# Attention with decay: the order of transposes, scores and projection steps within a head

## The chip, the cores and the metric

The kernel runs on one core of a Trainium2 chip, as one program. The metric is the time of one execution on the device, in microseconds (us). A profile of one execution shows five engines: TensorE (PE in the rows; its weight loads stand apart as PEld), VectorE (DVE), ScalarE (ACT), GpSimd (POOL) and SyncE (SP), which here only issues transfers.

## The reference, cut to what matters

The program computes two blocks of a network for 1024 tokens of width 1024. The change lies in the last layer of the second block, in its attention with decay ("forgetting attention"): 16 heads of width 64, causal, with a learned decay that is added to the scores.

```python
def forgetting_attention(u, k, v, cum):
    q = u.reshape(B, S, FOX_HEADS, FOX_HEAD_DIM)
    ...
    def block(args):
        qi, ci, s0 = args
        logits = jnp.einsum('bqhd,bkhd->bhqk', qi, k,
                            preferred_element_type=jnp.float32) * scale
        logits = logits + (ci[..., :, None] - cum_k[:, :, None, :])
        qpos = s0 + jnp.arange(Q_BLOCK)
        mask = kpos[None, :] <= qpos[:, None]
        logits = jnp.where(mask[None, None], logits, -jnp.inf)
        p = jax.nn.softmax(logits, axis=-1)
        return jnp.einsum('bhqk,bkhd->bqhd', p.astype(v.dtype), v)
```

The queries, keys and gates of each head come from projections of the layer's input `x`, by columns of `w_in` and `w_kv_shared`.

## The kernel before, in words

All matrices are split into a high and a low part, so that one product of two of them is three matmuls (`mm3`, L437 to L439). Every engine has its own program, written out by hand in a fixed order, and the programs meet at semaphores. Nothing schedules anything at run time: an engine whose next instruction has to wait stands still, and all that is behind it waits too.

The loop over the 16 heads (stage "fox") runs on TensorE, ScalarE and VectorE side by side. A head has eight tiles of 128 queries, `qt` 0 to 7. Tile `qt` sees `qt + 1` blocks of 128 keys, in one chunk of up to 512 keys for tiles 0 to 3 and in two for tiles 4 to 7. A tile goes through this chain:

1. `scores` (TensorE, L1767, L1768, and L1770 for the causal mask) writes a chunk to one of three PSUM banks.
2. `row_max` (VectorE, L3121) adds the decay, finds the extreme of each row and writes the logits to `tmp`, of which there are two, one for even and one for odd tiles.
3. `exps` (ScalarE, L1907, `tmp<-tmp,mx`) takes the exponential in place and its row sum.
4. `flips` (TensorE, L1781) transposes the exponentials block by block, one matmul each, to one of two PSUM banks.
5. `flip_hi` (ScalarE, `ET.._hi<-ps`) and `flip_lo` (VectorE, L2426, `ET.._lo<-ps`) split the transposed block.
6. `values` (TensorE, L1799) multiplies two tiles at a time (pair p is tiles 2p and 2p + 1) with the values, once both are split. `other_half` (ScalarE, `tmp<-ps 64x256`) and `add` (VectorE, L2429) bring the sum to `Y`, and free the bank of the next pair.

Between these TensorE has other work to fill its time: projection steps for later heads, `fill(n)` in units of one step, three matmuls of 512 columns. Eight steps make a half tile, a head has 24 steps, and the table `FILL` says how many stand at each of ten places: behind the scores of tiles 0 to 7, and around the last transposes. Heads 14 and 15 have less to project and go by `FILL_LAST`. A half tile for keys and queries (`kq`) is brought in by three ScalarE instructions (`project`) and three on VectorE, the last of them a cast (L3093); one for a gate takes one and one. Of these, the one finished at the end of the head before is brought in at tile 0, the first of this head at tile 2, the second from tile 5 on. In even heads from 2 on the one at tile 0 is a `kq` one; the one at tile 2 is `kq` in all even heads and a gate in odd ones. GpSimd splits the next weights (L881, `whi`, and L883, `wlo`) when a panel comes free, once of these at the end of each odd head.

The orders that matter are the three loops over `qt`, one on each engine, which must agree with each other.

Of the kernel before, what the change touches and what calls it, by code (L numbers as in the profile page):

```python
# [99 lines left out]
def chunks_of(qt):  # L100
    return 1 if qt < 4 else 2
# [62 lines left out]


MERGE_SPLITS = (4, 6, 8, 10)
FILL = (4, 4, 4, 3, 2, 1, 2, 1, 2, 1)
FILL_LAST = (3, 3, 3, 3, 2, 2, 0, 0, 0, 0)
VORDER = (tuple(range(8)), (2, 3, 4, 5, 6, 7, 0, 1))

# [46 lines left out]
def build(nc, d, out, upto=99, dbg=None):  # L217
    ctx = ExitStack()
    with ctx:
# [798 lines left out]
        def pe_program(pe):  # L1018
# [124 lines left out]
            if on("gates"):  # L1143
# [14 lines left out]
                def fill(n):  # L1158
                    for _ in range(n):
                        next(tiles, None)  # L1160
# [554 lines left out]
            if on("fox"):  # L1715
# [29 lines left out]
                def half_tiles(h):  # L1745
                    for kind, x, s in projections(h):
                        yield from half_tile(half_panel(kind, x), s)
# [69 lines left out]
                for h in range(FOX):  # L1817
                    steps = half_tiles(h)
                    share = FILL if h < FOX - 2 else FILL_LAST

                    def fill(n):
                        for _ in range(n):
                            next(steps, None)

                    for qt in range(8):
                        scores(h, qt)
                        if qt == 7:
                            fill(share[qt])
                        if qt:
                            flips(h, qt - 1)  # L1830
                        if qt < 7:
                            fill(share[qt])
                        if qt in (3, 5, 7):
                            values(h, qt // 2 - 1)
                        elif qt == 1 and h:
                            values(h - 1, 3)
                    fill(share[8])
                    if h == FOX - 1:
                        next(ahead)
                    flips(h, 7)  # L1840
                    fill(share[9])
                    if h == FOX - 1:
                        next(ahead)
# [61 lines left out]
        def act_program(act):  # L1905
# [167 lines left out]
            if on("mla"):  # L2073
# [18 lines left out]
                def exps(t):  # L2092
                    x = 8 * (t // 8 % 2) + t % 8
                    act.wait_ge(S("ml_max"), t + 1)
                    copy(tmp3[t % 3][:, :], tmp3[t % 3][:, :], S("ml_e"), ACT.Exp, bias=neg_max[:, x:x + 1], accum_out=row_sum[:, x:x + 1])
# [247 lines left out]
            if on("fox"):  # L2343
                def project(kind, x, s):

                    c = slice(HALF * s, HALF * s + HALF)
                    m = half_panel(kind, x)
                    if s:
                        panels_done(act, "fox", 25, 0, m)
                    else:  # L2350
                        act.wait_ge(S("fx_half"), m + 1)
                    g = ps[:, (6 + s) * HALF:(7 + s) * HALF]
                    if kind == "kq":
                        j = x % 2
                        if x < 2:
                            act.wait_ge(S("fx_vst"), 16)
                        else:
                            act.wait_ge(S("fx_x"), CHUNKS * (x - 1))
                        copy(K1[j][0:64, c], g[0:64, :], S("fx_kqa"))
                        copy(Q1[j][64:128, c], g[64:128, :], S("fx_kqa"), scale=64 ** -0.5)  # L2360
                        act.wait_ge(S("fx_kqa"), 4 * x + 2 * s + 1)
                        copy(K1[j][64:128, c], f32(K1[j][0:64, c]), S("fx_ka2"))
                    elif kind == "mq":
                        copy(Qm[0][0][:, c], g, S("mq_hi"))
                    else:
                        act.wait_ge(S("gate_log"), 4)
                        if x >= 2:
                            act.wait_ge(S("fx_yg"), x - 1)
                        copy(SG[x % 2][:, c], g, S("fx_sig"), ACT.Tanh, scale=0.5)

                def exps(h, qt):
                    x = 8 * (h % 2) + qt
                    act.wait_ge(S("fx_x"), CHUNKS * h + first_chunk(qt) + chunks_of(qt))
                    e = tmp[qt % 2][:, 0:P * qt + P]
                    copy(e, e, S("fx_e"), ACT.Exp, scale=-1.0, bias=neg_max[:, x:x + 1], accum_out=row_sum[:, x:x + 1])

                def flip_hi(h, qt):
                    p = qt // 2
                    if 4 * h + p >= 2:
                        act.wait_ge(S("fx_out"), 3 * (4 * h + p) - 5)  # L2380
                    for x in range(chunks_of(qt)):
                        n = CHUNKS * h + first_chunk(qt) + x
                        k0, k1 = 4 * x, min(4 * x + 4, qt + 1)
                        act.wait_ge(S("fx_t"), n + 1)
                        b = (3 + n % 2) * HALF
                        if qt == 0 and h:
                            act.wait_ge(S("row_stored"), CUM_STORED + 16 * (h - 1))
                            copy(inv_rows, ps[0:8, b + P:b + 2 * P], S("fx_inv"))
                        copy(ET[p % 2][0][:, k0:k1, P * (qt % 2):P * (qt % 2) + P], ps[:, b:b + P * (k1 - k0)].rearrange("p (k q) -> p k q", q=P), S("fx_hi"))

                def other_half(h, p):
                    o = others(64 * (h % 2))
                    r = slice(64 * (h % 2), 64 * (h % 2) + 64)
                    act.wait_ge(S("fx_out"), 3 * (4 * h + p) + 1)
                    copy(other[r, :], ps[o, 5 * HALF:5 * HALF + CTX], S("fx_out"))

                for x in (("kq", 0, 0), ("kq", 0, 1), ("gate", 0, 0), ("gate", 0, 1)):
                    project(*x)
                for h in range(FOX):
                    before = projections(h - 1)[2:] if h else []  # L2400
                    mine = projections(h)[0:2]
                    for qt in range(8):
                        if qt:
                            flip_hi(h, qt - 1)
                        exps(h, qt)
                        if qt in (3, 5, 7):
                            other_half(h, qt // 2 - 1)
                        elif qt == 1 and h:
                            other_half(h - 1, 3)
                        if qt == 0:  # L2410
                            for x in before:
                                project(*x)
                        if qt in (2, 5) and mine:
                            project(*mine[qt // 4])
                    flip_hi(h, 7)
                other_half(FOX - 1, 3)
# [6 lines left out]
        def dve_program(dve):  # L2423
# [655 lines left out]
            if on("fox"):  # L3079
# [69 lines left out]
                for h in range(FOX):  # L3149
                    before = projections(h - 1)[2:] if h else []  # L3150
                    mine = projections(h)[0:2]
                    for qt in range(8):
                        for x in range(chunks_of(qt)):
                            row_max(h, qt, x)
                        for x in range(chunks_of(qt - 1) if qt else 0):
                            flip_lo(h, qt - 1, x)
                        if qt in (3, 5, 7):
                            add(h, qt // 2 - 1)
                        elif qt == 1 and h:
                            add(h - 1, 3)  # L3160
                        if qt == 0:
                            for x in before:
                                project(*x)
                        if qt == 2 and mine:
                            project(*mine[0])
                        if qt >= 5 and mine:
                            kind, which, half = mine[1]
                            if kind == "kq":
                                keys_queries(which, half, qt - 5)
                            elif qt == 5:  # L3170
                                project(kind, which, half)
                        if qt == 7 and h % 2 == 0 and h:
                            gate(h // 2 - 1)
                    x = slice(8 * (h % 2), 8 * (h % 2) + 8)
                    dve.wait_ge(S("fx_e"), 8 * h + 8)
                    if h:
                        dve.wait_ge(S("fx_inv"), 2 * h)
                    nc.vector.reciprocal(inv_sum[:, x], row_sum[:, x]).then_inc(S("fx_inv"), 1)
                    for x in range(2):
                        flip_lo(h, 7, x)  # L3180
# [148 lines left out]
```

## Time and profile before

| | |
|---|---|
| median of 3 executions | 3017.0 us (3014.71 to 3017.37) |
| the profiled execution | 3021.57 us |
| its span, first to last instruction | 3019.8 us |
| TensorE busy | 2916.5 us, 97% of the span |
| VectorE, ScalarE, GpSimd busy | 49%, 31%, 37% |
| granted TensorE clock, mean | 0.991 of full speed |

The span is the profile's own time, and 1.8 us of the execution lie around it. TensorE is busy nearly always, so its instructions set the time; where it stands still, the chain that it waits for does.

### The profile page before, as it was taken

How to read it: one execution, taken by the hardware profiler on the slowest of the kernel's cores; microseconds unless marked ns; L12 is line 12 of the kernel's file. 1: busy time of each engine (PE TensorE's matmuls, PEld its weight loads, DVE VectorE, ACT ScalarE, POOL GpSimd, SP SyncE). 2: the span in 40 equal slices, each digit the busy share in tenths (PEclk: the TensorE clock that was granted, in tenths of full speed). 3: DMA queues.
4: the chain of work that ended last, by engine and by line, in shares of the span. 5: the costliest groups of instructions: out<-in, count | busy, mean ns of one | idle time of the engine just before them, and what ended most of it. 6: DMA issues, size and time to landing. Idle time of an engine off the chain costs nothing. (4 is left out here: it accounts for less than half of the span.)

```text
span 3019.8 us, 37184 instructions
## 1 busy us (share of the span) xinstructions
PE 2916.5 (97%) x14772; PEld 2424.8 (80%) x14772; DVE 1491.6 (49%) x2202; ACT 925.3 (31%) x1628; POOL 1108.4 (37%) x585
## 2 busy tenths in 40 slices
PE   7999999999999999999999999999899999999997
PEld 3877778888887888888888887788788888887786
DVE  5842237887644313122133444445626666664545
ACT  4122226675113101010011111420326555653411
POOL 1332351111586434444443443234343233322241
PEclk9999999999999999999999999999999999999998
DMA  5534574331533111111111111111142222221111
GB/s 239 188 129 142 191 235 137 86 89 48 190 122 112 50 49 49 49 50 49 50 49 49 49 63 56 42 42 49 54 165 63 73 66 71 69 71 50 37 49 63
DMA packets 123821, 263.00 MB, mean 87 GB/s; under 512 B 48476, under 2 KB 74540, under 8 KB 119424
## 3 DMA queue, kind: packets, MB, share of 16 engines
q1 hardware_dynamic: 123648, 260.57, 26.2%
q8 instruction: 124, 2.03, 0.3%
q14 instruction: 49, 0.40, 0.0%
HBM read 215.97 MB, written 46.06 MB: 87 GB/s over the span
## 5 line engine op out<-in xcount | busy, mean ns | idle before, releaser
L881 POOL TENSOR_TENSOR whi<-raw,onesf 128x1024 fp32r<-128x1024 f32 x187 | 362.0, 1936 | 1313.1 <-PE ps L439 1208.9
L437 PE MATMUL ps<-Hb_hi,whi 128*128 128x512 f32 x1424 | 572.6, 402 | 10.3 <-DVE Y L2846 5.9
L439 PE MATMUL ps<-Hb_hi,wlo 128*128 128x512 f32 x1424 | 556.0, 390 | 0.0
L438 PE MATMUL ps<-Hb_lo,whi 128*128 128x512 f32 x1424 | 554.9, 390 | 0.0
L883 POOL TENSOR_TENSOR wlo<-raw,whi 128x1024 fp32r<-128x1024 f32 x187 | 499.3, 2670 | 14.6
L437 PEld LDWEIGHTS ps<-Hb_hi,whi 128*128 128x128 f32 x1424 | 267.9, 188 | 62.6 <-issue 8.3
L439 PEld LDWEIGHTS ps<-Hb_hi,wlo 128*128 128x128 f32 x1424 | 267.2, 188 | 57.7
L438 PEld LDWEIGHTS ps<-Hb_lo,whi 128*128 128x128 f32 x1424 | 268.3, 188 | 48.0
L1907 ACT ACTIVATE tmp<-ps 64x256 f32<-64x256 f32 (+3 forms) x112 | 61.8, 552 | 535.9 <-PE ps L439 465.1
L1907 ACT ACTIVATE tmp<-tmp,mx 128x1280 f32<-128x1280 f32 (+2 forms) x192 | 187.1, 974 | 79.8 <-DVE mx L3121 50.3
L439 PE MATMUL ps<-Uhi,wlo 128*128 128x512 f32 x512 | 199.2, 389 | 0.0
L437 PE MATMUL ps<-Uhi,whi 128*128 128x512 f32 x512 | 199.2, 389 | 0.0
L438 PE MATMUL ps<-Ulo,whi 128*128 128x512 f32 x512 | 199.2, 389 | 0.0
L2429 DVE TENSOR_TENSOR tmp<-tmp 128x1024 f32<-128x1024 f32 x44 | 86.1, 1957 | 184.1 <-ACT tmp L1907 183.7
L2793 DVE SCALAR_TENSOR_TENSOR X<-ps,modx,X 128x1024 f32<-128x1024 f32 x32 | 41.1, 1283 | 256.6 <-PE ps L439 256.6
L437 PE MATMUL ps<-Yb_hi,whi 128*128 128x512 f32 (+1 forms) x408 | 153.8, 377 | 0.0
L438 PE MATMUL ps<-Yb_lo,whi 128*128 128x512 f32 (+1 forms) x408 | 153.6, 377 | 0.0
L439 PE MATMUL ps<-Yb_hi,wlo 128*128 128x512 f32 (+1 forms) x408 | 153.6, 377 | 0.0
L437 PE MATMUL ps<-Hhi,whi 128*128 128x512 f32 x384 | 151.8, 395 | 0.4 <-ACT ql L1907 0.2
L438 PE MATMUL ps<-Hlo,whi 128*128 128x512 f32 x384 | 149.6, 390 | 0.0
L439 PE MATMUL ps<-Hhi,wlo 128*128 128x512 f32 x384 | 149.5, 389 | 0.0
L438 PEld LDWEIGHTS ps<-Ulo,whi 128*128 128x128 f32 x512 | 96.1, 188 | 20.1
(468 smaller groups left out, 5832.4 us busy)
## 6 DMA issues: line engine op xcount, KB each, us to landing
raw<-in_w SPq DMA_DIRECT2D x197, 512.0 KB, 3.5
adas<-in_ada SPq DMA_DIRECT2D x16, 1024.0 KB, 4.9
raw<-in_w SPq DMA_DIRECT2D x44, 256.0 KB, 3.7
adaE<-in_ada SPq DMA_DIRECT2D x4, 2048.0 KB, 23.2
gate_d<-gst SPq DMA_DIRECT2D x16, 512.0 KB, 2.8
v_d<-VS SPq DMA_DIRECT2D x2, 4096.0 KB, 14.2
ncB<-cum_d SPq DMA_DIRECT2D x16, 512.0 KB, 3.6
Vx<-v_d SPq DMA_DIRECT2D x16, 512.0 KB, 3.8
```

What stands on the lines that cost most here:

```text
L437: nc.tensor.matmul(o, wh, xh, start=start, stop=False)
L438: nc.tensor.matmul(o, wh, xl, start=False, stop=False)
L439: return nc.tensor.matmul(o, wl, xh, start=False, stop=stop)
L881: nc.gpsimd.tensor_tensor(whi[b][:, 0:w], raw[b][:, 0:w], onesf[:, 0:1].to_broadcast([P, w]), ALU.mult).then_inc(S("split_hi"), 1)
L883: nc.gpsimd.tensor_tensor(wlo[b][:, 0:w], raw[b][:, 0:w], f32(whi[b][:, 0:w]), ALU.subtract).then_inc(S("split"), 1)
L1907: nc.scalar.activation(dst, src, func, **kw).then_inc(sem, 1)
L2429: nc.vector.tensor_tensor(o, a, b, op).then_inc(sem, 1)
L2793: nc.vector.scalar_tensor_tensor(X1[:, k, :], g, modx[:, 40 + k:41 + k], X1[:, k, :], ALU.mult, ALU.add).then_inc(free, 1)
```

## The change

The transposes of tile `t` stood behind the scores of tile `t + 1`, and the projection steps of that place behind them. Now the table `FLIPPED` places them: those of tiles 0 and 1 stand together behind the scores and the steps of tile 1, those of tiles 2 and 3 together behind the scores and the steps of tile 3. Behind the scores of tile 4 stand no transposes. Those of tiles 4, 5, 6 and 7 stay where they were. ScalarE and VectorE follow the same order, and on ScalarE the exponential of tiles 1 to 4 now comes ahead of the `flip_hi` that stand at the same place. `FILL` is redistributed (24 steps, as before); `FILL_LAST` stays.

```diff
--- before.py
+++ after.py
@@ -164,7 +164,8 @@
 
 
 MERGE_SPLITS = (4, 6, 8, 10)
-FILL = (4, 4, 4, 3, 2, 1, 2, 1, 2, 1)
+FILL = (3, 4, 3, 4, 2, 1, 2, 1, 2, 2)
+FLIPPED = {1: (0, 1), 3: (2, 3), 5: (4,), 6: (5,), 7: (6,)}
 FILL_LAST = (3, 3, 3, 3, 2, 2, 0, 0, 0, 0)
 VORDER = (tuple(range(8)), (2, 3, 4, 5, 6, 7, 0, 1))
 
@@ -1824,11 +1825,11 @@
 
                     for qt in range(8):
                         scores(h, qt)
-                        if qt == 7:
+                        if qt < 4 or qt == 7:
                             fill(share[qt])
-                        if qt:
-                            flips(h, qt - 1)
-                        if qt < 7:
+                        for t in FLIPPED.get(qt, ()):
+                            flips(h, t)
+                        if 4 <= qt < 7:
                             fill(share[qt])
                         if qt in (3, 5, 7):
                             values(h, qt // 2 - 1)
@@ -2400,9 +2401,12 @@
                     before = projections(h - 1)[2:] if h else []
                     mine = projections(h)[0:2]
                     for qt in range(8):
-                        if qt:
-                            flip_hi(h, qt - 1)
-                        exps(h, qt)
+                        if qt < 5:
+                            exps(h, qt)
+                        for t in FLIPPED.get(qt, ()):
+                            flip_hi(h, t)
+                        if qt >= 5:
+                            exps(h, qt)
                         if qt in (3, 5, 7):
                             other_half(h, qt // 2 - 1)
                         elif qt == 1 and h:
@@ -3152,8 +3156,9 @@
                     for qt in range(8):
                         for x in range(chunks_of(qt)):
                             row_max(h, qt, x)
-                        for x in range(chunks_of(qt - 1) if qt else 0):
-                            flip_lo(h, qt - 1, x)
+                        for t in FLIPPED.get(qt, ()):
+                            for x in range(chunks_of(t)):
+                                flip_lo(h, t, x)
                         if qt in (3, 5, 7):
                             add(h, qt // 2 - 1)
                         elif qt == 1 and h:
```

TensorE, head 2, from the last two matmuls of the values of pair 0 to the first projection step of tile 4 (`Vx` values, `K` keys, `Q` queries, `mrow` the causal mask, `Hb` and `w` the projections). Before:

```order
L1799 MATMUL ps<-ETa_hi,Vx_191 128x128
L1799 MATMUL ps<-ETa_lo,Vx_191 128x128
L1767 MATMUL ps<-K_0_187,Q_0_185 128x512
L1768 MATMUL ps<-K_0_189,Q_0_185 128x512
L1767 MATMUL ps<-K_0_187,Q_0_185 128x128
L1768 MATMUL ps<-K_0_189,Q_0_185 128x128
L1770 MATMUL ps<-mrow_60,identr 128x128
L1781 MATMUL ps<-ident,tmp 128x128 x4
L437 MATMUL ps<-Hb_hi,whi 128x512
```

And now, in the same head, where all line numbers are a little higher:

```order
L1782 MATMUL ps<-ident,tmp 128x128 x7
L1800 MATMUL ps<-ETa_hi,Vx_191 128x256
L1800 MATMUL ps<-ETa_lo,Vx_191 128x256
L1800 MATMUL ps<-ETa_hi,Vx_191 128x128
L1800 MATMUL ps<-ETa_lo,Vx_191 128x128
L1768 MATMUL ps<-K_0_187,Q_0_185 128x512
L1769 MATMUL ps<-K_0_189,Q_0_185 128x512
L1768 MATMUL ps<-K_0_187,Q_0_185 128x128
L1769 MATMUL ps<-K_0_189,Q_0_185 128x128
L1771 MATMUL ps<-mrow_60,identr 128x128
L438 MATMUL ps<-Hb_hi,whi 128x512
```

The four transposes of tile 3 moved from behind the scores of tile 4 to ahead of the values, where they join the three of tile 2.

VectorE, same head, from `row_max` of tile 3 to that of tile 4 (`ISA` is `row_max` or its second part, `ETb_lo` is `flip_lo`, `Y` is `add`). Before:

```order
L3121 ISA tmp,mx<-ps,ncB 128x512
L3121 ISA mx 128x1
L2426 TENSOR_TENSOR ETb_lo<-ps,ETb_hi 128x3x128
L2429 TENSOR_TENSOR Y_170<-ps,tmp 64x256
L3121 ISA tmp,mx<-ps,ncB 128x512
L3121 ISA mx 128x1
L3121 ISA tmp,mx<-ps,ncB,mx 128x128
L3121 ISA mx 128x1
L2426 TENSOR_TENSOR ETb_lo<-ps,ETb_hi 128x4x128
```

Now:

```order
L3125 ISA tmp,mx<-ps,ncB 128x512
L3125 ISA mx 128x1
L2430 TENSOR_TENSOR ETb_lo<-ps,ETb_hi 128x3x128
L2430 TENSOR_TENSOR ETb_lo<-ps,ETb_hi 128x4x128
L2433 TENSOR_TENSOR Y_170<-ps,tmp 64x256
L3125 ISA tmp,mx<-ps,ncB 128x512
L3125 ISA mx 128x1
L3125 ISA tmp,mx<-ps,ncB,mx 128x128
L3125 ISA mx 128x1
```

The low half of tile 3 moved from behind `row_max` of tile 4 to ahead of it and of the `add` of pair 0.

ScalarE, same head, from the key and query copies of tile 2's place to the exponential of tile 4 (`128x512` and `128x640` with `mxf` are the exponentials of tiles 3 and 4, `64x256` is `other_half`). Before:

```order
L1907 ACTIVATE K_1_188<-K_1_188 64x512
L1907 ACTIVATE ETb_hi<-ps 128x3x128
L1907 ACTIVATE tmp,mxf<-tmp,mx 128x512
L1907 ACTIVATE tmp<-ps 64x256
L1907 ACTIVATE ETb_hi<-ps 128x4x128
L1907 ACTIVATE tmp,mxf<-tmp,mx 128x640
```

Now:

```order
L1908 ACTIVATE K_1_188<-K_1_188 64x512
L1908 ACTIVATE tmp,mxf<-tmp,mx 128x512
L1908 ACTIVATE ETb_hi<-ps 128x3x128
L1908 ACTIVATE ETb_hi<-ps 128x4x128
L1908 ACTIVATE tmp<-ps 64x256
L1908 ACTIVATE tmp,mxf<-tmp,mx 128x640
```

The exponential of tile 3 went ahead of the high half of tile 2, and the high half of tile 3 ahead of `other_half`.

## Rows read from the trace of the kernel before

**Rows 1.** View of windows, head 6: length, busy time (xinstructions), PE clock, DMA share, GB/s.

```profile
2434.64:2465.00 30.36, 30.36 (x183) 26.66 (x181) 20.83 (x50) 18.90 (x43) 11.72 (x8) 1.00 0.26 79
```

**Rows 2.** View of waits, stretch of all heads: us in total, times, longest.

```profile
PE ps L1781 <- ACT tmp L1907: 4.1, 4, 1.2
```

**Rows 3.** Timeline of TensorE, head 6, tiles 4 and 5: start, duration, row, count.

```profile
2449.20 0.28 PE L1799 MATMUL ps<-ETa_hi,Vx 128*128 128x256 f32 x1
...
2449.60 0.45 PE L1767 MATMUL ps<-K,Q 128*128 128x512 f32 x1
...
2450.40 0.62 PE L1781 MATMUL ps<-ident,tmp 128*128 128x128 f32 x4
2450.78 0.47 PE L437 MATMUL ps<-Hb_hi,whi 128*128 128x512 f32 x1
2451.09 0.39 PE L438 MATMUL ps<-Hb_lo,whi 128*128 128x512 f32 x1
...
2452.25 0.40 PE L1767 MATMUL ps<-K,Q 128*128 128x512 f32 x1
...
2453.01 0.72 PE L1781 MATMUL ps<-ident,tmp 128*128 128x128 f32 x5
```

**Rows 4.** Timeline of ScalarE and VectorE, same stretch; in brackets idle before and releaser.

```profile
2449.81 0.38 ACT L1907 ACTIVATE tmp<-ps 64x256 f32<-64x256 f32 x1 [0.61 <-PE ps L1799]
...
2450.22 0.42 DVE L2429 TENSOR_TENSOR Y<-ps,tmp 64x256 f32<-64x256 f32 x1 [1.40 <-ACT tmp L1907]
...
2450.56 0.67 DVE L3121 CUSTOM_DVE_ANT_0 tmp<-ps,ncB 128x512 f32<-128x512 f32 x1
...
2451.12 0.60 ACT L1907 ACTIVATE ETb_hi<-ps 128x512 fp32r<-128x512 f32 x1 [0.93 <-PE ps L1781]
...
2451.75 0.69 DVE L2426 TENSOR_TENSOR ETb_lo<-ps,ETb_hi 128x512 fp32r<-128x512 f32 x1
2451.78 0.83 ACT L1907 ACTIVATE tmp<-tmp,mx 128x640 f32<-128x640 f32 x1
```

**Rows 5.** Timeline, exponentials and the transposes behind them, head 6 and head 15.

```profile
2458.57 1.05 ACT L1907 ACTIVATE tmp<-tmp,mx 128x896 f32<-128x896 f32 x1
...
2459.85 0.93 PE L1781 MATMUL ps<-ident,tmp 128*128 128x128 f32 x7
...
2708.72 0.40 ACT L1907 ACTIVATE tmp<-tmp,mx 128x128 f32<-128x128 f32 x1 [2.17 <-DVE mx L3121]
...
2709.26 0.33 PE L1781 MATMUL ps<-ident,tmp 128*128 128x128 f32 x1 [0.76 <-ACT tmp L1907]
```

**Rows 6.** Timeline of all engines, start of head 6.

```profile
2434.64 0.23 PE L1767 MATMUL ps<-K,Q 128*128 128x128 f32 x1
...
2434.93 0.45 PE L437 MATMUL ps<-Hb_hi,whi 128*128 128x512 f32 x1
...
2435.21 0.40 PE L438 MATMUL ps<-Hb_lo,whi 128*128 128x512 f32 x1
2435.44 0.39 PE L439 MATMUL ps<-Hb_hi,wlo 128*128 128x512 f32 x1
...
2436.93 2.40 POOL L883 TENSOR_TENSOR wlo<-raw,whi 128x1024 fp32r<-128x1024 f32 x1
...
2438.38 1.23 DVE L3093 CAST K<-K 64x512 fp32r<-64x512 f32 x1
...
2439.64 0.43 DVE L3121 CUSTOM_DVE_ANT_0 tmp<-ps,ncB 128x256 f32<-128x256 f32 x1
...
2440.11 0.51 ACT L1907 ACTIVATE tmp<-tmp,mx 128x256 f32<-128x256 f32 x1 [1.19 <-DVE mx L3121]
```

**Rows 7.** Timeline, head 6: scores of tile 2, a later cast, exponential of tile 3.

```profile
2442.86 0.39 PE L1767 MATMUL ps<-K,Q 128*128 128x384 f32 x1
...
2447.20 0.42 DVE L3093 CAST K<-K 64x512 fp32r<-64x512 f32 x1
...
2448.38 0.72 ACT L1907 ACTIVATE tmp<-tmp,mx 128x512 f32<-128x512 f32 x1 [0.50 <-DVE mx L3121]
```

## The prediction

> **What bounds the kernel now.** I read the windows first, by head. In head 6 TensorE is busy for all of its 30.36 us, at a granted clock of 1.00, while VectorE is busy 20.83 and ScalarE 18.90 [rows 1]. So a head lasts as long as the list of TensorE's instructions, and a change in order can help in two ways only: by taking away a wait of TensorE, or by making the same matmuls cheaper. Then the view of waits: over all 16 heads the transposes make TensorE wait for an exponential four times, 4.1 us in all [rows 2]. That is all that a better order could take from this wait. It can lose far more, since each of the 16 heads can get a new wait. So I went through the chains behind each wait of the new order, with the starts of one head from the timeline, and asked which instruction TensorE would reach before its input is there.
>
> A first price is needed: how soon behind an exponential its transposes can start. In head 15 TensorE really waited: the exponential started at 2708.72 and took 0.40, the transposes started at 2709.26, so 0.14 us behind its end. In head 6 the exponential of tile 6 started at 2458.57 and took 1.05, so its transposes could have started at 2459.76, and did at 2459.85 [rows 5]: on time, with 0.09 us to spare. The loop is tight already.
>
> **The change, place by place.** The transposes of tiles 5, 6 and 7 and their surroundings stay, so I cost four places.
>
> Tile 4, every head. Before, TensorE starts the transposes of tile 3 at 2450.40 and those of tile 4 at 2453.01, 2.61 us later, with two projection steps and the scores of tile 5 between them [rows 3]. Now the values of pair 0 (2449.20 to 2449.60, 0.40) and the scores of tile 4 (2449.60 to 2450.40, 0.80) stand between them as well [rows 3], and the mask's matmul is followed by a projection matmul, 0.06 (below). TensorE is there after 2.61 + 0.40 + 0.80 + 0.06 = 3.87 us.
>
> The chain that it then waits for begins at the same transposes of tile 3, which before had nothing to do with it. From 2450.40 it takes 0.72 to the high half (2451.12), which takes 0.60, and the low half starts at 2451.75, 1.35 behind the transposes [rows 3, 4]. Now `other_half` comes behind this high half, from 1.35 to 1.73; the low half takes 0.69, to 2.04; only then `add`, and `row_max` of tile 4 starts 0.34 behind the start of `add` (2450.22 to 2450.56), so at 2.07 + 0.34 = 2.41. From there it is 1.22 to the exponential (2450.56 to 2451.78) [rows 4]: 3.63. The exponential takes 0.83 and the step to the transposes 0.14: 4.60. TensorE is there at 3.87 and waits 0.73 us. In 16 heads this is 11.7 us, the largest term. Both ends: 0, if the scores of tile 4 were in fact not late for anything, which the rows exclude as long as `row_max` of tile 4 stands behind the low half and `add`; and 1.0 if each handover of the chain costs 0.05 more than where I read it. Behind the waiting transposes stand a projection step, the values of pair 1 and the scores of tile 6; nothing on the other engines runs ahead enough to make the time good, since they wait for these very transposes.
>
> Tile 1, even heads from 2 on. `row_max` of tile 1 stands on VectorE behind the three instructions that bring in keys and queries. In head 6 the last of these, a cast, starts at 2438.38 and takes 1.23, where the cast at 2447.20 takes 0.42 [rows 6, 7]. The difference is GpSimd: its `wlo` runs from 2436.93 to 2439.33, and the cast ends 0.28 behind it, at 2439.61 [rows 6]. GpSimd's two instructions hang on the last projection step of the head before, which still stands right ahead of the scores of tile 0. I take it that the cast, though it may start up to 0.7 us earlier by the table's extra step at the end of a head, is still held until `wlo` ends. Then `row_max` of tile 1 starts at 5.00 us from the head's start and the exponential at 5.47 as now; it takes 0.51, and the transposes of tile 1 can start at 6.12. TensorE gets there, with 0.29 for the scores of each of tiles 0 and 1, seven steps of 0.69 (a matmul follows the next by 0.23, 2435.21 to 2435.44), two masks at 0.06 and 0.15 for the transposes of tile 0 with the row sums, at 5.68 [rows 6]; the 0.29 for tile 1 and the 0.15 are estimates from tile 0 and from 0.38 for four transposes [rows 3]. The wait is 0.44, in heads 2 to 12 together 2.6 us. Head 14 goes by `FILL_LAST`, with one step less: 1.1 us. Ends: 0, if the cast is not held, and 0.7 for each.
> The Trainium skill says why, in SBUF — State Buffer, Who interferes with whom: a VectorE instruction that uses two ports and one of GpSimd take the shared pair of ports as a lock, and the later one stands still until the other has ended. The two casts agree with that. By this rule the sum holds the 3.7 us of this place; without it the casts would take 0.42 and the sum would be that much less.
>
> Tile 3, even heads. From the scores of tile 2 (2442.86) to the exponential of tile 3 (2448.38) it is 5.52, and 0.72 + 0.14 to its transposes: 6.38 [rows 7]. TensorE took 6.34 to the values of pair 0 (2449.20) [rows 3, 7]; now the transposes of tile 1 are no longer in it (two of 0.11), two masks add 0.12 and one handover of 0.06 falls away: 6.18. A wait of 0.20 in seven heads, 1.4 us, and 0.9 in head 14 with its shorter table. In odd heads a gate is brought in, one instruction for three, and there is none.
>
> The masks, every head. The last matmul of a tile's scores has 128 columns. Behind it the first matmul of a projection step takes 0.28 until the next (2434.93 to 2435.21), where it is 0.23 from the second to the third [rows 6]: some 0.06 that a matmul of 128 columns doesn't cover. Before, transposes stood behind four of these masks; now projection steps do, at tiles 1, 2, 3 and 4. Four times 0.06 in 16 heads would be 3.8 us; the transposes have the same exposed load in part, so I take 3 (ends 0 and 3.8).
>
> What is removed. Putting transposes together saves nothing that I can find: four take 0.38 and the matmul behind them 0.31 instead of 0.23 [rows 3, 6], 0.46 in all or 0.115 each, as if each were charged alone. The wait of head 15 for its first exponential, 0.76 [rows 5], goes, as four steps now lie ahead. No transfer is issued by these loops, and GpSimd and SyncE follow semaphores with time to spare; a later row of sums reaches them some 2 us later in a head of 30.
>
> Sum: 11.7 + 2.6 + 1.1 + 1.4 + 0.9 + 3.0 - 0.8 = 19.9 us. The profiled execution took 3021.57 (span 3019.8, 1.8 around it) and would take 3041; its time is 4.6 over the median of 3017.0, to which I add the same sum: 3037 us, 0.66% more.
>
> **The rivals.**
> The chain is longer than I read, and the new waits are not the last. The spare 0.09 us at tile 6 [rows 5] goes as soon as one copy is late, and then tile 6 waits in every head as well; with 0.25 there (4 us) and 1.0 instead of 0.73 at tile 4 (4.3 us) the time is 3045. For it: each engine's program is one queue, and every handover has its price. Against it: behind tile 4 all engines follow the same transposes, as before. Chance 0.2.
> The casts are not held at tile 1, as their start moves off GpSimd's work: 3.7 us less, 3033. Against it: GpSimd starts from the same projection step as before. Chance 0.1.
> The waits don't come, since ScalarE and VectorE, with 11 and 9 us of idle time in a head [rows 1], catch up. Then 3.0 - 0.8 remain, 3019, which can't be told from no change (0.2%, 6 us, is about what can be). Against it: idle time is no slack where a chain runs through it. Chance 0.07.
> It gets faster. The mechanism is the 0.08 that a matmul behind a group of transposes pays (0.31 against 0.23) [rows 3, 6]: if that is paid once for a group, two groups fewer in 16 heads save 2.6 us, and with the 4.1 us of waits [rows 2] gone, 6.7 us: 3010. It decides where the new waits stay under 0.4 us for each head. Against it: of those waits only the 0.76 stands at a place that changes, and tile 4's wait alone is above that bound. Chance 0.03.
>
> **How the numbers follow.** The forecast as worked out has 0.6, the rivals 0.2, 0.1, 0.07 and 0.03. The predicted time is 3037. The range runs from 3028, which takes in the casts that are not held and masks at nothing together with a fifth off the largest term, to 3047, which takes in the longer chain with the masks at 3.8 and is rounded up. Faster by over 0.2%: 0.03; within: 0.07; slower: 0.9.
>
> **What the profile would show.** Right: heads of some 31.3 us (odd) and 31.9 (even) instead of 30.4; in the view of waits, TensorE for an exponential at the transposes, 16 waits near 0.7 at tile 4, seven near 0.4 at tile 1, seven near 0.2 at tile 3; casts at tile 1 of even heads that end 0.28 behind `wlo`; projection matmuls at 0.28 behind masks. Wrong: no wait at tile 4, or `row_max` of tile 4 that starts within 2 us of the transposes of tile 3. The forecast fails if the distance between the transposes of tiles 3 and 4 is under 4 us.

## The result and the profile after

The changed kernel takes 3043.55 us (median of 4 executions, 3041.77 to 3047.2), the kernel before 3017.18 (4 executions, 3014.71 to 3022.37). The ratio is 1.0085, 95% interval 1.0071 to 1.0100: slower by 26 us, by 21 to 30. Forecast were 3037 us, with a range of 3028 to 3047, and 0.9 for slower.

The profiled execution took 3042.88 us with a span of 3041.1, 21.3 more than that of before. All of it lies in the heads; the rest of the span is 1.3 shorter. The view of windows over them, from the first scores of head 0 to the first matmul of the next stage (length, busy time of PE, PEld, DVE, ACT and POOL, then clock and transfers):

```profile
2251.55:2762.46 510.91, 491.83 (x2880) 424.03 (x2878) 318.17 (x771) 280.22 (x634) 147.56 (x108) 1.00 0.22 67
```

Before, this stretch took 488.29 us, from 2254.41 to 2742.70. It grew by 22.6. I call it the stage below and measure every kernel by it as well as by the ratio, since what lies outside it differs by some us from one profiled execution to another. Heads 6 and 7 of the changed kernel in the same view:

```profile
2439.62:2471.51 31.89, 31.23 (x183) 26.75 (x181) 21.33 (x51) 18.85 (x42) 11.51 (x8) 1.00 0.26 76
2471.51:2502.99 31.48, 30.73 (x182) 26.80 (x181) 18.61 (x49) 16.55 (x38) 7.22 (x6) 1.00 0.20 59
```

Head 6 took 30.36 us with TensorE busy throughout [rows 1]; now it takes 31.89 with 31.23 busy, and the odd head 7 takes 31.48 with 30.73 busy. ScalarE works no longer than before (18.85 against 18.90), and the granted clock is 1.00 as it was. TensorE runs the same matmuls and stands still between them. Its busy time grows as well (30.73 against 30.35 in head 7): the row of a matmul goes on after the next could have started, so a part of each wait counts as busy. The view of waits over the heads says what TensorE waits for:

```profile
PEld ps L1782 <- ACT tmp L1908: 26.3, 43, 1.4
...
PE ps L1782 <- ACT tmp L1908: 17.5, 30, 1.2
```

The wait for an exponential at the transposes grew from 4.1 us in 4 places [rows 2] to 17.5 in 30. The row of weight loads (PEld) shows the same waits once more, by the idle time of the loads; the two are not added. The largest one, at tile 4, in the timeline of TensorE for head 7:

```profile
2485.23 0.93 PE L1782 MATMUL ps<-ident,tmp 128*128 128x128 f32 x7
2485.91 0.36 PE L1800 MATMUL ps<-ETa_hi,Vx 128*128 128x256 f32 x1
...
2486.40 0.44 PE L1768 MATMUL ps<-K,Q 128*128 128x512 f32 x1
...
2488.61 0.39 PE L1768 MATMUL ps<-K,Q 128*128 128x512 f32 x1
...
2489.30 0.22 PE L1771 MATMUL ps<-mrow,identr 128*128 128x128 f32 x1
2490.28 0.77 PE L1782 MATMUL ps<-ident,tmp 128*128 128x128 f32 x5 [0.75 <-ACT tmp L1908]
```

From the mask (2489.30) to the transposes of tile 4 (2490.28) it is now 0.98 us, where an undisturbed mask is followed after 0.06; the 0.75 in brackets is only the part in which no matmul is busy. The wait costs 0.92 us. What it waited for, on ScalarE and VectorE:

```profile
2485.81 1.03 ACT L1908 ACTIVATE ETb_hi<-ps 128x384 fp32r<-128x384 f32 x2 [1.43 <-PE ps L1782]
2486.87 0.38 ACT L1908 ACTIVATE tmp<-ps 64x256 f32<-64x256 f32 x1
2489.30 0.83 ACT L1908 ACTIVATE tmp<-tmp,mx 128x640 f32<-128x640 f32 x1 [2.05 <-DVE mx L3125]
...
2486.34 1.23 DVE L2430 TENSOR_TENSOR ETb_lo<-ps,ETb_hi 128x384 fp32r<-128x384 f32 x2 [2.81 <-ACT ETb_hi L1908]
2487.60 0.43 DVE L2433 TENSOR_TENSOR Y<-ps,tmp 64x256 f32<-64x256 f32 x1
2488.06 0.69 DVE L3125 CUSTOM_DVE_ANT_0 tmp<-ps,ncB 128x512 f32<-128x512 f32 x1
```

The low halves of tiles 2 and 3 run as one row from 2486.34 to 2487.57; only then `add` (2487.60), `row_max` of tile 4 (2488.06) and its exponential (2489.30), and 0.98 behind its start the transposes. The scores of tile 4 had been there since 2487.4.

At tile 1 of an even head (GpSimd, VectorE, ScalarE, TensorE of head 6):

```profile
2441.90 2.40 POOL L884 TENSOR_TENSOR wlo<-raw,whi 128x1024 fp32r<-128x1024 f32 x1
...
2443.16 1.43 DVE L3097 CAST K<-K 64x512 fp32r<-64x512 f32 x1
2444.62 0.42 DVE L3125 CUSTOM_DVE_ANT_0 tmp<-ps,ncB 128x256 f32<-128x256 f32 x1
...
2445.09 0.51 ACT L1908 ACTIVATE tmp<-tmp,mx 128x256 f32<-128x256 f32 x1 [2.26 <-DVE mx L3125]
...
2445.74 0.44 PE L1782 MATMUL ps<-ident,tmp 128*128 128x128 f32 x2 [0.20 <-ACT tmp L1908]
```

GpSimd's `wlo` ends at 2444.30, the cast at 2444.59, and behind it `row_max`, the exponential and the transposes of tile 1, which are 0.43 us late (0.47 behind the row of sums where it was 0.10 in odd heads, and 0.20 to the values instead of 0.14). The cast started 3.54 us from the head's start instead of 3.74, and lasted 1.43 instead of 1.23 [rows 6], so it ended at the same place in the head.

At tile 3, TensorE of head 6, then GpSimd, VectorE and TensorE of head 8:

```profile
2453.77 1.15 PE L1782 MATMUL ps<-ident,tmp 128*128 128x128 f32 x7
2454.67 0.36 PE L1800 MATMUL ps<-ETa_hi,Vx 128*128 128x256 f32 x1
...
2515.29 0.73 POOL L898 TENSOR_TENSOR Y<-Y,rs 64x256 f32<-64x256 f32 x1 [7.61 <-DMA acc<-inv_d]
...
2515.57 0.73 DVE L3097 CAST K<-K 64x512 fp32r<-64x512 f32 x1
...
2517.94 0.66 PE L1782 MATMUL ps<-ident,tmp 128*128 128x128 f32 x4 [0.31 <-ACT tmp L1908]
```

The seven transposes of tiles 2 and 3 take 0.90 us in head 6, up to the values at 2454.67, and 0.68 in odd heads: 0.22 late. In head 8 the cast that stands ahead of `row_max` of tile 3 took 0.73 instead of 0.42: it ends at 2516.30, again 0.28 behind an instruction of GpSimd (a multiplication of the head before, 2515.29 to 2516.02). The transposes of tile 3 wait longer there and show 0.31 us of idle time.

### The profile page after: what moved, and what is told of

It is laid out like the page before. It is cut to its first block, busy times and chain, and to the rows that moved or that the text cites. A ratio compares the mean times of both kernels' runs of the same rounds, so it can differ in the third digit from the quotient of the medians.

```text
span 3041.1 us, 37184 instructions
## 1 busy us (share of the span) xinstructions
PE 2926.3 (96%) x14772; PEld 2428.2 (80%) x14772; DVE 1496.9 (49%) x2202; ACT 924.0 (30%) x1628; POOL 1106.6 (36%) x585
## 4 chain that ended last, share of the span: by engine, by line
PE 80%; DVE 9%; ACT 4%; issue 3%; DMA 2%; POOL 1%; SPq 0%; ACTq 0%; DVEq 0%; POOLq 0%
PE ps L438 23%; PE ps L440 22%; PE ps L439 22%; PE ps L1375 2%; ACT tmp L1908 2%; PE ps L1800 2%; PE ps L1359 2%; PE ps L1782 2%; DVE tmp L3125 1%; DMA raw<-in_w 1%; DVE Z L2433 1%; DVE mx L2877 1%; PE ps L1768 1%; PE ps L1769 1%; DVE acc L2457 1%
## 5 line engine op out<-in xcount | busy, mean ns | idle before, releaser
L898 POOL TENSOR_TENSOR Y<-Y,rs 64x256 f32<-64x256 f32 x30 | 22.4, 745 | 255.4 <-DMA acc<-inv_d 255.4
```

## The experiments

Each kernel is timed against the kernel before on the same chip and in the same batch; the changed kernel's ratio is that of the section above. "Stage" is the stretch defined above, against 488.3 us before and 510.9 as changed.

| kernel | ratio (95%) | stage, us | odd head 7, even head 6, us |
|---|---|---|---|
| before | | 488.3 | 30.35, 30.36 |
| changed | 1.0085 (1.0071 to 1.0100) | 510.9 | 31.48, 31.89 |
| table_only | 0.9994 (0.9985 to 1.0003) | 488.5 | 30.36, 30.36 |
| pair_01 | 1.0015 (1.0006 to 1.0024) | 493.2 | 30.48, 30.91 |
| pair_23 | 1.0048 (1.0034 to 1.0062) | 503.5 | 31.38, 31.16 |
| step_to_tile4 | 1.0045 (1.0031 to 1.0059) | 500.5 | 30.78, 31.18 |
| low3_late | 1.0063 (1.0050 to 1.0077) | 506.4 | 31.16, 31.66 |
| cast_behind_max1 | 1.0044 (1.0031 to 1.0058) | 506.0 | 31.48, 31.45 |
| low_keys_from_psum | 1.0064 (1.0050 to 1.0078) | 508.0 | 31.49, 31.72 |
| all_three | 1.0006 (0.9997 to 1.0015) | 491.6 | 30.52, 30.52 |
| late_in_14 | 1.0028 (1.0016 to 1.0041) | 497.1 | 30.35, 30.34 |

The theory was the one of the prediction: the pairs close three chains, and TensorE waits for them at the transposes of tiles 4, 1 and 3. The rivals were that the table of steps does it, that any pair makes everything behind it late, and for each chain that something else in it is what holds.

In a window's line, the first time is the length of the head and the second TensorE's busy time, as above.

**The table alone.** The kernel before with one line changed:

```diff
-FILL = (4, 4, 4, 3, 2, 1, 2, 1, 2, 1)
+FILL = (3, 4, 3, 4, 2, 1, 2, 1, 2, 2)
```

> The kernel before with nothing changed but the table of projection steps (3, 4, 3, 4, 2, 1, 2, 1, 2, 2). Theory (the chains that the pairs close cost the time): no pair, so no chain closes; tile 0 and tile 2 meet their transposes 0.7 us sooner, where they had over 1.3 us to spare; TensorE waits for exponentials stay near 4 us in all, heads stay at 30.4 us, ratio 1.000 (within 0.002). Rival (the redistributed steps cost the time, by leaving some tile short): waits in ordinary heads, heads over 31 us, ratio 1.005 or more.

```profile
2431.08:2461.44 30.36, 30.36 (x183) 26.64 (x182) 21.24 (x50) 18.88 (x42) 11.53 (x8) 1.00 0.28 79
```

Ratio 0.9994, which can't be told from 1; head 6 takes 30.36 us, all of it busy (view of windows). The steps alone are not the cause. The pairs with the old table were not run.

**One pair at a time.** In both, a tile without a pair goes back to its old place; the core of the first:

```diff
-FLIPPED = {1: (0, 1), 3: (2, 3), 5: (4,), 6: (5,), 7: (6,)}
+FLIPPED = {1: (0, 1), 3: (2,), 4: (3,), 5: (4,), 6: (5,), 7: (6,)}
+STEPS_FIRST = (0, 1, 2)
...
-                        if qt < 4 or qt == 7:
+                        if qt in STEPS_FIRST or qt == 7:
                             fill(share[qt])
```

and for the second `{1: (0,), 2: (1,), 3: (2, 3), ...}` with `STEPS_FIRST = (0, 3, 4)`; ScalarE's exponentials follow the same table.

> The changed kernel with the transposes of tiles 2 and 3 put back behind the scores of tiles 3 and 4; those of tiles 0 and 1 stay together. Theory: only the wait at tile 1 of even heads stays (0.43 us in six heads, 1.1 in head 14), head 15 keeps its gain of 0.9, and some 0.1 us a head goes for one group behind which values stand: 4 us more than before, ratio 1.0015; odd heads at 30.5 us, even ones at 30.9. Rival (any pair makes the later tiles late): waits at tiles 3 and 4 as well, ratio over 1.004.

> The changed kernel with the transposes of tiles 0 and 1 put back; those of tiles 2 and 3 stay together. Theory: the wait at tile 4 stays whole (0.9 us in odd heads, 0.6 in even ones, 12.4 in all), that at tile 3 of even heads loses the 0.2 us that tile 1's transposes now fill again (2.6 in all), 0.1 us a head for the group: 17 us more than before, ratio 1.0055; odd heads at 31.4 us. Rival (the two pairs help to make each other's waits): clearly less than the whole cost less what the other pair shows.

Windows of heads 6 and 7, first of pair_01:

```profile
2435.03:2465.94 30.91, 30.70 (x182) 26.65 (x181) 21.41 (x50) 18.88 (x42) 11.67 (x8) 1.00 0.27 78
2465.94:2496.42 30.48, 30.48 (x183) 26.71 (x182) 18.57 (x49) 16.64 (x38) 7.23 (x6) 1.00 0.21 61
```

and of pair_23:

```profile
2439.67:2470.83 31.16, 30.67 (x182) 26.73 (x181) 21.24 (x50) 18.86 (x42) 11.54 (x8) 1.00 0.27 77
2470.83:2502.21 31.38, 30.63 (x182) 26.76 (x181) 18.65 (x49) 16.54 (x38) 7.21 (x6) 1.00 0.22 59
```

The heads came out as worked out, to 0.02 us: 30.91 and 30.48 for the first pair, 31.38 for an odd head of the second. The stage grew by 4.9 us (4 expected) and by 15.2 (17 expected). Together that is 20.1 of 22.6. The rest lies at tile 3 of even heads, which costs 1.1 us in all in pair_23 and 4.0 in the changed kernel. Of these 2.9, some 1.3 are the interplay that was expected, since with both pairs the two transposes of tile 1 no longer fill time ahead of tile 3. The other 1.6 come from the cast at tile 2, which takes 0.42 us in every even head of pair_23, but 0.71 to 0.97 in heads 2, 8, 10 and 14 of the changed kernel; other small items make up for 0.4. The first pair's effect does not reach the later tiles, but for 0.11 us at tile 4 of head 14: rival refuted.

**More work in the gap.** One step from the end of the head to tile 4:

```diff
-FILL = (3, 4, 3, 4, 2, 1, 2, 1, 2, 2)
+FILL = (3, 4, 3, 4, 3, 1, 2, 1, 2, 1)
```

> The changed kernel with one projection step moved from the end of the head to tile 4: table (3, 4, 3, 4, 3, 1, 2, 1, 2, 1). Theory (at tile 4 TensorE is simply there too soon, by 0.92 us in odd and 0.63 in even heads): 0.69 us of work in that gap leaves 0.23 in odd heads and nothing in even ones, 10.6 us less than the changed kernel: ratio to before 1.004; odd heads at 30.8 us. Rival (the chain behind tile 4 is short everywhere and the wait moves on to tile 6, which had 0.09 us to spare): waits of over 0.4 us at tile 6, ratio over 1.006.

```profile
2437.64:2468.82 31.18, 30.96 (x183) 26.66 (x181) 20.99 (x50) 18.88 (x43) 11.68 (x8) 1.00 0.26 77
2468.82:2499.60 30.78, 30.71 (x183) 26.79 (x181) 18.63 (x49) 16.57 (x39) 7.22 (x6) 1.00 0.21 61
```

Odd heads take 30.78 us (30.8 expected), and the stage is 10.4 shorter (10.6 expected). The view of waits for ordinary heads shows nothing at tile 6. The ratio, 1.0045, fits the 1.004. So the wait at tile 4 is a gap that work can fill, and it doesn't move on.

**What the chain to tile 4 consists of.** On VectorE the low half of tile 3 alone goes back behind `row_max` of tile 4:

```diff
-                        for t in FLIPPED.get(qt, ()):
+                        for t in {3: (2,), 4: (3,)}.get(qt, FLIPPED.get(qt, ())):
                             for x in range(chunks_of(t)):
                                 flip_lo(h, t, x)
```

> The changed kernel, but on VectorE the low half of tile 3 stands behind row_max of tile 4 again; all else as changed. Theory (the wait at tile 4 is the length of the chain from tile 3's transposes, in which this low half stands ahead of add and row_max): add needs only other_half, which ends 1.73 us behind tile 3's transposes, so row_max of tile 4 starts at 2.1 to 2.2 instead of 2.5, and the wait at tile 4 falls by about 0.35 us in each of 16 heads, 5.6 in all: ratio 1.0066, odd heads at 31.1 us. Rival (the wait hangs on ScalarE, where the high half of tile 3 stands ahead of other_half and of the exponential): no change, odd heads at 31.5 us, ratio 1.0085.

Head 7, the transposes of tiles 2 and 3 and those of tile 4 on TensorE, `add` and `row_max` of tile 4 on VectorE:

```profile
2486.35 0.93 PE L1782 MATMUL ps<-ident,tmp 128*128 128x128 f32 x7
...
2491.08 0.76 PE L1782 MATMUL ps<-ident,tmp 128*128 128x128 f32 x5 [0.43 <-ACT tmp L1908]
...
2488.40 0.43 DVE L2433 TENSOR_TENSOR Y<-ps,tmp 64x256 f32<-64x256 f32 x1 [0.39 <-ACT tmp L1908]
2488.86 0.69 DVE L3125 CUSTOM_DVE_ANT_0 tmp<-ps,ncB 128x512 f32<-128x512 f32 x1
```

`row_max` starts 2.51 us behind the transposes of tiles 2 and 3, and 2.83 before (2485.23 to 2488.06): 0.32 sooner, as much as the head is shorter (31.16 against 31.48). The low half was part of the chain. The stage is 4.5 us shorter, where 5.6 were expected: in even heads the wait at tile 4 falls by only some 0.2 us. The rest of that wait remains (0.60 in odd heads, 0.35 to 0.46 in even ones). That it is the two high halves ahead of `other_half` on ScalarE is read from the order of its rows, and no run isolates it.

**The cast at tile 1.** First moved behind `row_max` of tile 1, then replaced by an instruction that reads PSUM:

```diff
+                        if qt == 1 and before and before[0][0] == "kq":
+                            project(*before[0], (2,))
...
-                                project(*x)
+                                project(*x, range(2))
```

> The changed kernel, but the cast of the keys that are brought in at tile 0 stands behind row_max of tile 1 on VectorE. Theory (TensorE waits at tile 1 for the exponential, that for row_max, and that for this cast, which GpSimd holds): row_max of tile 1 starts at 3.6 us of an even head instead of 5.0, the transposes of tile 1 could start at 4.7, TensorE is there at 5.6: no wait at tile 1, 0.43 us less in six heads and 1.1 in head 14, 3.7 in all, ratio 1.0073; even heads at 31.4 us (head 4) instead of 31.9, odd ones as they are. Rival (the wait at tile 1 comes from row sums or the bank of tile 0's transposes): the wait stays.

VectorE of head 6 from `row_max` of tile 1 on, and the head's window:

```profile
2439.82 0.42 DVE L3125 CUSTOM_DVE_ANT_0 tmp<-ps,ncB 128x256 f32<-128x256 f32 x1
...
2440.28 1.10 DVE L3097 CAST K<-K 64x512 fp32r<-64x512 f32 x1
...
2436.41:2467.86 31.45, 30.96 (x183) 26.78 (x182) 20.97 (x51) 18.73 (x42) 11.52 (x8) 1.00 0.27 77
```

`row_max` of tile 1 starts 3.41 us from the head's start instead of 5.00, no even head from 2 to 12 waits at tile 1, and head 6 takes 31.45 us, 0.44 less. The stage is 4.9 shorter, where 3.7 was expected; most of the rest is that in heads 2, 8 and 10 the casts ahead of tile 3 took 0.42 us in this execution. The ratio came out lower than expected (1.0044 against 1.0073). The stage alone gives 1.0058, and that is the upper end of the interval; the remainder lies outside the heads and has no cause here that I know.

Then the instruction that reads PSUM:

```diff
+                    if part == 3:
+                        nc.vector.tensor_tensor(K2[j][64:128, c], g[0:64, :], f32(K1[j][0:64, c]), ALU.subtract).then_inc(S("fx_kd2"), 1)
...
-                def project(kind, x, s, parts=range(3)):
+                def project(kind, x, s, parts=(0, 3, 1)):
```

> The changed kernel, but at tiles 0 and 2 the cast that copies the low keys to the other partitions within SBUF is replaced by a subtraction that reads PSUM, as the one of the first copy does; same place in the queue, one input from SBUF. Theory (the cast is long since GpSimd's wlo holds the ports that both use): the new instruction takes 0.69 us everywhere, also where wlo runs beside it, and row_max of tile 1 starts by 4.4 us of an even head: no wait at tile 1. Tile 3 gets 0.27 more where the cast was 0.42 and less where it was 0.9. Ratio 1.0075. Rival (what is long there is the read or write of the keys, whatever the instruction): it takes 1.4 us, and the wait at tile 1 stays at 0.4. The Trainium skill (SBUF — State Buffer, Who interferes with whom) counts an instruction with one input from SBUF as not using the shared pair, which agrees with the theory.

The view of the keys' tile over all heads (durations in ns, minimum, median, maximum), then VectorE and GpSimd at the start of head 6:

```profile
L3089 DVE TENSOR_TENSOR K<-ps,K x15: 683/685/686, 2259.7 to 2701.8; 64x512 fp32r<-64x512 f32 x15
L3099 DVE CAST K<-K x14: 420/421/423, 2278.2 to 2689.2; 64x512 fp32r<-64x512 f32 x14
...
2440.56 0.68 DVE L3089 TENSOR_TENSOR K<-ps,K 64x512 fp32r<-64x512 f32 x1
2441.28 0.69 DVE L3095 SCALAR_TENSOR_TENSOR Q<-ps,Q 64x512 fp32r<-64x512 f32 x1
2442.00 0.42 DVE L3127 CUSTOM_DVE_ANT_0 tmp<-ps,ncB 128x256 f32<-128x256 f32 x1
...
2440.16 2.40 POOL L884 TENSOR_TENSOR wlo<-raw,whi 128x1024 fp32r<-128x1024 f32 x1
```

The new instruction, L3089, takes 683 to 686 ns in all 15 places, and in head 6 it runs from 2440.56 to 2441.24 inside GpSimd's `wlo` (2440.16 to 2442.56). The cast in the same place took 1.43 us in head 6 of the changed kernel, and up to 1.56 in its other heads. So it is the kind of instruction that is held, not the keys. By the Trainium skill (SBUF — State Buffer, Who interferes with whom) the shared pair of ports is locked for a whole instruction, and reading PSUM with one input from SBUF doesn't need it; these rows agree. No wait at tile 1 is left in heads 2 to 12, and 0.23 us in head 14. At tile 3 heads 2 to 12 now each show 0.27 us of idle time (0.19 in head 0, 0.94 in head 14), as the new instruction is 0.26 longer than a free cast; so the stage is only 2.9 us shorter than the changed kernel's.

**All together.** The step, the low half, and the casts of tiles 0 and 2 behind `row_max` of tiles 1 and 3; the last in code:

```diff
+                        if qt == 3 and mine and mine[0][0] == "kq":
+                            project(*mine[0], (2,))
```

> The changed kernel with the step moved to tile 4, the low half of tile 3 behind row_max of tile 4, and the casts of tiles 0 and 2 behind row_max of tiles 1 and 3. Theory (three chains make the waits, and 0.21 us a head is the price of the order itself): no waits in ordinary heads, all of them at 30.6 us; with what is left in head 14 and head 15's gain, 3.5 us more than before, ratio 1.001, not faster than before. Rival (there is a further chain behind these): heads over 31 us, ratio over 1.003.

```profile
2432.09:2462.61 30.52, 30.52 (x183) 26.71 (x181) 20.75 (x50) 18.71 (x43) 11.58 (x8) 1.00 0.27 80
2462.61:2493.13 30.52, 30.52 (x183) 26.71 (x181) 18.55 (x49) 16.59 (x39) 7.24 (x6) 1.00 0.21 61
```

Odd and even heads take 30.52 us and TensorE is busy in all of it. The stage is 3.3 us over that of before, of 22.6. There is no further chain in ordinary heads; head 14 still waits at tiles 3 and 4, and head 15 at tile 4. What remains in an ordinary head, 0.16 us, is the price of the order itself (below). The ratio is 1.0006 (0.9997 to 1.0015), not to be told from before.

**Where waits are left to win.** The kernel before waits at its transposes only in heads 14 and 15. Head 14 alone was changed, in the kernel before:

```diff
+FILL_14 = (3, 3, 3, 1, 1, 1, 2, 1, 1, 0)
...
-                    before = projections(h - 1)[2:] if h else []
-                    mine = projections(h)[0:2]
+                    before = projections(h - 1)[2 - (h == FOX - 1):] if h else []
+                    mine = projections(h)[0:2 - (h == FOX - 2)]
```

> The kernel before, pairs undone, with head 14 alone changed: the second half tile of keys and queries that it projects is brought in at tile 0 of head 15 instead of tile 5 of head 14, and its 16 steps stand as 3, 3, 3, 1, 1, 1, 2, 1, 1, 0, so that some are left for tiles 6 and 7. Theory (a wait of TensorE is where the time of this stage can be won, and only heads 14 and 15 have any): head 14 loses its waits at tile 7's scores and at the transposes of tiles 6 and 7 (0.7, 1.3 and 1.2 us) and goes from 27.9 to about 24.8 us; ratio 0.999, at the edge of what 5 rounds tell. Rival (the same work is late wherever the steps stand): head 14 stays over 27 us.

The expectation was wrong, and the kernel got slower: ratio 1.0028, the stage 8.8 us longer, head 14 at 27.32 us instead of 27.90. Two things were overlooked. Tiles 3 and 4 of head 14, now with one step each, got waits of their own (1.32 and 0.81 us of idle time). And there is a queue of transfers that I had not looked at. SyncE's issues, then VectorE and TensorE at the start of head 15 (in brackets the idle time and what ended it):

```profile
2709.72 0.34 SPq L472 DMA_DIRECT2D raw<-in_w  x1
2710.11 0.43 SPq L817 DMA_DIRECT2D ncB<-cum_d  x1
...
2714.68 0.29 DVE L3122 CUSTOM_DVE_ANT_0 tmp<-ps,ncB 128x128 f32<-128x128 f32 x1 [5.94 <-DMA ncB<-cum_d]
...
2715.57 0.47 PE L1782 MATMUL ps<-ident,tmp 128*128 128x128 f32 x1 [7.63 <-ACT tmp L1908]
```

The last step of a half tile frees a weight panel. It now stands at the end of the head, so GpSimd splits the next panel later (its `whi` starts at 2704.50, in the kernel before at 2696.23), the load of raw weights that waits for GpSimd is issued at 2709.72 (before: 2700.61), and behind it in the same queue stands the decay row of head 15 (`ncB`, 2710.11; before: 2703.40). `row_max` of tile 0 had to wait for it until 2714.68, and TensorE for 7.63 us.

## Why the prediction held, step by step

Tile 4. The chain was forecast at 4.60 us behind tile 3's transposes and TensorE at 3.87. In head 7 those transposes began 0.32 behind 2485.23, so the transposes of tile 4 started 4.73 behind them, and TensorE would have been there at 3.81. The wait is 0.92 us in all odd heads and 0.60 to 0.66 in even ones: 12.4 us in all, 11.7 forecast. That the total came so near is in part luck, since odd heads lie above the 0.73 us of the forecast and even ones below it. The difference between them was to be read before the change. `add` and `row_max` of tile 4, in head 7 of the kernel before, then in head 6 of the changed kernel:

```profile
2480.57 0.43 DVE L2429 TENSOR_TENSOR Y<-ps,tmp 64x256 f32<-64x256 f32 x1 [1.75 <-ACT tmp L1907]
2481.03 0.69 DVE L3121 CUSTOM_DVE_ANT_0 tmp<-ps,ncB 128x512 f32<-128x512 f32 x1
...
2456.25 0.41 DVE L2433 TENSOR_TENSOR Y<-ps,tmp 64x256 f32<-64x256 f32 x1
2456.58 0.67 DVE L3125 CUSTOM_DVE_ANT_0 tmp<-ps,ncB 128x512 f32<-128x512 f32 x1
```

The prediction took 0.34 us from `add` to `row_max` out of head 6 [rows 4] and used it for all heads. In odd heads it is 0.46, before the change as after it: there `row_max` starts only when `add` has ended, in even heads 0.08 before that. From the low half of tile 3 to `row_max` it is 1.18 us in odd heads of the changed kernel and 0.94 in even ones, so the whole chain takes 4.73 and 4.52 us (4.46 in head 0), and TensorE gets there at 3.81 and at 3.86 to 3.91. In odd heads `add` writes the other half of the partitions; whether that is the reason no run isolates. pair_23 isolates the wait at tile 4, low3_late shows a link of it.

Tile 1. The cast held until `wlo` ends, though it started earlier: 0.43 a head in heads 2 to 12 and 1.1 in head 14, 3.7 in all, 3.7 forecast. The two cast experiments show that the cast is the link.

Tile 3. Forecast 0.20 in seven heads and 0.9 in head 14, 2.3 in all. Measured 0.22 in heads 4, 6 and 12 and 0.15 in head 0; but 0.5 to 0.8 in heads 2, 8 and 10, and 1.2 in head 14: 4.0. The step that was mis-sized took the cast at tile 2 as free, 0.42 us; GpSimd holds that one too in some heads (0.92 us in head 2, 0.73 in head 8, 0.97 in head 10, 0.71 in head 14), where it still multiplies for the head before. This too stood in the trace of the kernel before, where the cast at tile 2 took 0.98, 0.86 and 1.00 us in heads 2, 4 and 10. Head 2, GpSimd and VectorE:

```profile
2325.59 0.74 POOL L897 TENSOR_TENSOR Y<-Y,rs 64x256 f32<-64x256 f32 x1 [7.83 <-DMA acc<-inv_d]
...
2325.64 0.98 DVE L3093 CAST K<-K 64x512 fp32r<-64x512 f32 x1
```

The prediction read the free one of head 6 [rows 7]. Which heads are hit differs from kernel to kernel, so this part of the cost is not fixed.

The masks and the groups. Forecast 3 us for masks alone and nothing for the groups. Measured 0.21 us in head 7 beside its wait, 3.4 in the stage, but the account was incomplete: projection steps behind masks pay 0.06, yet no longer the 0.09 behind transposes, which the two groups of values pay instead (1.93 for those of pair 3 against 1.85, 0.49 for pair 0 against 0.41). Joining groups also made the transposes themselves longer: in odd heads the two groups of tiles 0 and 1 took 0.15 and 0.14 us and their joined one takes 0.36, those of tiles 2 and 3 took 0.25 and 0.38 and now 0.68, together 0.12 more. And transposes behind a wait take 0.52 where they took 0.48, which is why 0.16 or 0.17 is left of the 0.21 in all_three, where nothing waits. The sum was right, the split was not.

Head 15 gained 0.9 us, 0.8 forecast. Together 12.4 + 3.7 + 4.0 + 3.4 - 0.9 = 22.6, which is what the stage grew by; 19.9 were forecast. The ratio of the medians gives 25.6 (21 to 30), and 22.6 lies in that interval; for the remaining 3 there is nothing in the profile, whose own execution shows 1.3 less outside the heads. They may be chance: the kernel before took 3017.18 in the median of its 4 executions here, and 3020.6 to 3021.3 in the batches of the experiments, with 10 to 21 executions each.

Of the rivals, that of idle engines catching up fell: VectorE and ScalarE kept 10.6 and 13.0 us of idle time in head 6 (31.89 less 21.33 and 18.85) while TensorE waited for them. That of a chain with longer handovers was right in odd heads, with a chain 0.13 us longer where it had put 0.27 on tile 4, and wrong in even ones and on tile 6, where ordinary heads show no wait. The measured 3043.55 us lies nearer to its 3045 than to the 3037 of the forecast, but not by its mechanism. That of casts that are not held fell at tile 1 in every even head from 2 on, and that of a faster kernel with the waits and with the price of the joined groups.

## What to carry to other kernels

Before a block of work is put together on the engine that bounds, write down for each instruction behind it how soon the bound engine comes back for that result, and walk the other engines' queues from the same block to it. Here 3.87 us against 4.60 decided, although those engines were idle for a third of the time. A step that frees a buffer carries the transfers behind it: follow it through every queue up to the first load of something else, or head 15 waits 7.6 us for a row of decays. Read a price in more than one head before using it for all: the 0.34 us between two VectorE instructions and the 0.42 of a cast were true of the head that was read, and 0.46 and up to 1.00 stood a head or two further on. And moving one instruction in a helper's queue (a cast, a low half) can give back what reordering the bound engine costs.

## What the runs showed of the hardware

A VectorE cast from SBUF to SBUF, 64x512, takes 0.42 us alone. When it starts while GpSimd runs a 128x1024 `TENSOR_TENSOR`, it lasts until 0.28 to 0.29 us behind that instruction's end, whether it started earlier or later, in the changed kernel up to 1.56 us. A subtraction that reads PSUM and one SBUF input takes 0.683 to 0.686 us in all 15 places. I had expected that. I had not expected that the cast at tile 2 is held too, in heads 2, 8, 10 and 14, by GpSimd's short 64x256 multiplications, nor that a few hundredths of a us decide it: in head 10 the cast starts 0.05 us behind GpSimd's instruction and takes 0.97; in head 12 the cast starts at 2643.31 and takes its 0.42, and GpSimd's instruction of 2643.33 takes 1.00 instead of 0.73.

In a group of transposes each starts 0.11 us behind the one before, and the matmul behind the group starts 0.03 to 0.05 behind the last: three take 0.25 us, five 0.48, seven 0.68. That matmul then takes some 0.08 longer to its successor, once for a group. Two groups less per head gave nothing back, since each joined pair put 0.11 in place of one such 0.05, 0.12 us together, and projection steps behind masks paid 0.06 each.
